# Seven half products in place of eight for the first feed-forward layers, with the weight sums on GpSimd and all low parts on VectorE

## The chip, the cores and the metric

The kernel runs on one core of a Trainium2 chip. A core has a matrix engine (TensorE, PE in the rows; its weight loads are PEld), VectorE (DVE), ScalarE (ACT), GpSimd (POOL) and a queue that issues transfers (SP). Each engine works through its own instructions in order; semaphores hold one back until another has finished. The metric is the device time of one execution in microseconds, lower is better.

## The reference

The program is a small hybrid language model in float32: one block on 512 tokens, then two blocks on 528 (16 meta tokens are put in front), width 1024. Only the feed-forwards matter here. Cut to them:

```python
def sqrelu_mlp(hn, w1, w2):            # block 1: w1 1024 x 4096
    u = hn @ w1
    u = jnp.square(jax.nn.relu(u))
    return u @ w2

def swiglu(h, w_in, w_out):            # blocks 2 and 3: w_in 1024 x 5632
    gate, up = jnp.split(h @ w_in, 2, axis=-1)
    return (jax.nn.silu(gate) * up) @ w_out

h = h + sqrelu_mlp(rmsnorm(h, norm_ff_g[l]), w_ff1[l], w_ff2[l])
h = h + swiglu(rmsnorm_2(h, norm_ffn[i]), ffn_w_in[i], ffn_w_out[i])
```

Ahead of them stand a mixer (SSD and attention), a cross attention, a gated linear attention and a sparse attention.

## The kernel before

Activations lie transposed in SBUF: partitions are channels (8 tiles of 128), the free dimension is tokens. The residual is h. TensorE multiplies in a reduced float32 format, and to keep the accuracy every operand is split into a high and a low part; a product is three passes, high x high, high weights x low activations, low weights x high activations.

Weights come in 155 units of 128 x 2048 values (1 MB), in a fixed order of layers (table LAYERS). A feed-forward unit holds two output tiles of 128 channels: 8 input tiles x 256 columns. Each unit passes three stages in two alternating buffers: SP loads w_raw (when the split of two units earlier is done), ScalarE copies w_raw to w_hi (split_hi, L363), VectorE writes w_lo = w_raw - w_hi (split_lo, L370). While TensorE computes a unit, ScalarE and VectorE split the next one. In some layers of the middle GpSimd does the subtraction instead.

TensorE's work is pe_linear (L451): per unit and output tile 8 input tiles x 3 passes, into one of two PSUM slots (lin), with 512 tokens as one matmul, with 528 as two halves of 264. The semaphore lin_done counts tiles, lin_taken the slots read.

The three feed-forwards are cut into parts: ff1a, ff2a to ff1d, ff2d (4 units each, 512 tokens), up0a, dn0a, up0b, dn0b, up0c, dn0c (8, 4, 8, 4, 6, 4 units, 528 tokens) and up1a to dn1c (the same with 512). Behind each tile of ff1 ScalarE takes the relu out of PSUM (L1691), VectorE squares it (L1708), ScalarE and VectorE split it into x_hi and x_lo (L1693, L1710). In up, a unit holds one gate tile and one up tile: VectorE scales the gate (L2036), ScalarE applies silu (L2017), VectorE multiplies by the up tile (L2040), and the result is split (L2019, L2044). The second layers add to h (L546, L549).

The norm in front of a feed-forward is applied late: the layer that ends the preceding mixer (w_xo, g_out, a_out) adds to h tile by tile, and behind each tile ScalarE writes v_hi = gain x h (L602) and the squares (L614), VectorE writes v_lo (L619), GpSimd adds up the squares (L634). TensorE sums them over partitions, ScalarE and VectorE make the reciprocal root (L684, L703) beside the first unit, and it multiplies the results.

Of the kernel before, what the change touches and what calls it, by code (L numbers as in the profile page):

```python
# [17 lines left out]
F32 = mybir.dt.float32  # L18
# [55 lines left out]

class Linear:


    def __init__(self, row, unit0, tile0):
        self.name, self.units, self.kc, self.tpu, self.n, self.token_major = row
        self.unit0, self.tile0 = unit0, tile0  # L80
        self.tiles_end = tile0 + self.units * self.tpu
        self.last = row is LAYERS[-1]

# [46 lines left out]
def build(nc, weights, x_t, mem_t, meta_t, cols, consts, w_a2b, rel_t, rel_dram, out):  # L130
# [4 lines left out]
    with ctx:  # L135
# [118 lines left out]
        after_v.close()  # L254
        sb("v_place", [P, 2, KD, T2])

# [74 lines left out]

        def for_units(eng, L, body, peel=False):
# [4 lines left out]
            if L.units % 2 == 0 and L.units // 2 - peel >= 2 and not L.last:  # L337
# [17 lines left out]
        def split_hi(act, unit, i, tiles_before):  # L355


            s = unit % 2
# [6 lines left out]
        def split_lo(dve, unit, i, does):  # L365

            s = unit % 2
# [111 lines left out]
        def act_splits(act, L, after=None):  # L479
            def unit(j, i):  # L480
                next_hi(act, L, j, i)
                if after is not None and is_first(j, i):
                    after()
            for_units(act, L, unit, after is not None)
# [31 lines left out]
        def dve_residual(dve, L, scale=None, N=None, after=None, scale2=None, after_first=None, splits_from=0):  # L516
            base = KD * residual_layers.index(L.name)

            def unit(j, i):
# [4 lines left out]
                for m in range(L.tpu):  # L524
                    slot, before, n = L.tile(j, m, i)
# [31 lines left out]
        def act_residual(act, L, N, after=None, splits_from=0):  # L557
# [3 lines left out]
            def unit(j, i):  # L561
# [4 lines left out]
                for m in range(L.tpu):  # L566
                    t, par = (2 * i + j) * L.tpu + m, (j * L.tpu + m) % 2
# [12 lines left out]
        class LaterNorm:  # L580
            def __init__(self, n, eps, first, tile, gain, hi, lo, slots=(0,), square_scale=None, tokens=(),
                         k=KD, to=None, bank=0, roots=None):
# [7 lines left out]
                self.idx, self.bank = len(later_norms), bank  # L590
                self.tiles0 = sum(N.k for N in later_norms)
# [11 lines left out]

        def act_operand(act, N, t, par):
            if N.hi is not None:
# [1071 lines left out]

        def act_relu2(act, L, after=None):
            base = hidden0[L.name]

            def unit(j, i):
                next_hi(act, L, j, i)
                if after is not None and is_first(j, i):
                    after()
                for m in range(2):
                    slot, _, n = L.tile(j, m, i)
                    t = 4 * i + 2 * j + m
                    r, sq = tmp[:, m, 0:S1], tmp[:, 2 + m, 0:S1]
                    act.wait_ge(sem("lin_done"), n + 1)

                    nc.scalar.activation(r, psum_tile(slot, S1), ACT.Relu).then_inc(sem(f"lin_taken{slot}"), 1)  # L1691
                    act.wait_ge(sem("u_made"), base + t + 1)
                    nc.scalar.activation(one(u_hi, t, 0, S1), sq, ACT.Copy).then_inc(sem("u_hi"), 1)  # L1693
            for_units(act, L, unit, after is not None)

        def dve_relu2(dve, L, after=None):
            base = hidden0[L.name]

            def unit(j, i):
                next_lo(dve, L, j, i)  # L1700
                if after is not None and is_first(j, i):
# [1114 lines left out]
```

## Time and profile before

| | |
|---|---|
| median of 3 runs | 2085.11 us (2080.94 to 2085.74) |
| profiled execution | 2085.97 us, its span 2083.9 us |
| TensorE, weight loads busy | 2007.6 us (96%), 1719.7 us (83%) |
| VectorE, ScalarE, GpSimd busy | 1055.4 (51%), 745.3 (36%), 249.3 us (12%) |
| mean granted TensorE clock | 0.978 |
| weights moved | 155 x 1 MB, 84 GB/s over the span |

The span runs from the first to the last instruction. Busy means that at least one instruction of the engine is running; matmuls overlap each other, so their rate is read from their starts. In timelines a row is start, duration, engine, line, operation, output and inputs, and in brackets the idle time before it with what ended it. A row of a stretch is its window, its length, the busy us and instructions of TensorE, of its weight loads, of VectorE, ScalarE and GpSimd, then the granted clock, the share of the transfer engines and GB/s. The granted clock is the share of TensorE's full speed that it was given.

### The profile page before, as it was taken

The numbers are of one execution on the slowest core, as the hardware profiler recorded it, in microseconds if no ns is written. First come the engines' busy times: TensorE is split into PE (matmuls) and PEld (weight loads), VectorE is DVE, ScalarE is ACT, GpSimd is POOL, SyncE is SP. The second block draws the span as 40 slices with busy tenths as digits, with TensorE's granted clock in tenths as the row PEclk, the third lists the DMA queues.
The fourth block names the chain that finished last, engine by engine and source line by source line (L and its number), as shares of the span: only waits on it lengthen the run. The fifth ranks groups of instructions, "written<-read, shape, count | busy, mean of one in ns | idle before, by whom it ended". The sixth has DMA issues, their size and how long they took to land.

```text
span 2083.9 us, 28508 instructions
## 1 busy us (share of the span) xinstructions
PE 2007.6 (96%) x11498; PEld 1719.7 (83%) x11498; DVE 1055.4 (51%) x1353; ACT 745.3 (36%) x941; POOL 249.3 (12%) x208
## 2 busy tenths in 40 slices
PE   8999989999999999999999999999997899999996
PEld 6788766788888878999999999998884588888885
DVE  6668765544444544133443434346887444434435
ACT  4449734423132443223332222224444432222222
POOL 2012230200000210013200000001254010000001
PEclk9999999999999998998999999999998899999998
DMA  4223111222222221111222222223121022222221
GB/s 174 101 81 113 62 60 61 81 101 81 101 101 81 101 82 54 68 41 41 81 82 101 82 101 81 102 81 121 61 92 32 21 101 82 100 101 82 100 101 61
DMA packets 27823, 174.67 MB, mean 84 GB/s; under 512 B 4409, under 2 KB 4537, under 8 KB 7762
## 3 DMA queue, kind: packets, MB, share of 16 engines
q1 hardware_dynamic: 25680, 167.32, 22.6%
q0 software_dynamic: 1888, 5.90, 0.9%
q8 instruction: 71, 1.16, 0.2%
q14 instruction: 22, 0.18, 0.0%
q10 hardware_dynamic: 162, 0.10, 0.0%
HBM read 171.19 MB, written 4.78 MB: 84 GB/s over the span
## 4 chain that ended last, share of the span: by engine, by line
issue 58%; PE 30%; POOL 4%; DVE 3%; ACT 3%; DMA 1%; SPq 0%; POOLq 0%; DVEq 0%; ACTq 0%
PE lin L451 18%; POOL squares L634 3%; PE aux L2278 1%; PE aux L1307 1%; DMA w_raw<-in_weights 1%; PE lin L1509 1%; PE lin L1262 1%; ACT w_hi L363 1%; PE lin L2248 1%; PE aux L2262 1%; POOL w_lo L370 1%; PE aux L1291 1%; POOL r_t L1952 1%; PE aux L2126 1%; PE aux L2274 0%
## 5 line engine op out<-in xcount | busy, mean ns | idle before, releaser
L451 PE MATMUL lin<-v_hi,w_hi 128*128 128x264 f32 (+1 forms) x1664 | 555.6, 334 | 2.6 <-DVE gq_t L1772 1.4
L451 PE MATMUL lin<-v_hi,w_lo 128*128 128x264 f32 (+1 forms) x1664 | 553.3, 333 | 0.0
L451 PE MATMUL lin<-v_lo,w_hi 128*128 128x264 f32 (+1 forms) x1664 | 552.0, 332 | 0.0
L370 DVE TENSOR_TENSOR w_lo<-w_raw,w_hi 128x2048 fp32r<-128x2048 f32 (+1 forms) x144 | 328.5, 2281 | 184.5 <-ACT w_hi L363 184.2
L451 PE MATMUL lin<-x_hi,w_hi 128*128 128x512 f32 (+1 forms) x1160 | 408.4, 352 | 13.4 <-DVE tmp L546 6.5
L451 PE MATMUL lin<-x_hi,w_lo 128*128 128x512 f32 (+1 forms) x1160 | 406.7, 351 | 0.0
L451 PE MATMUL lin<-x_lo,w_hi 128*128 128x512 f32 (+1 forms) x1160 | 406.3, 350 | 0.0
L363 ACT ACTIVATE w_hi<-w_raw 128x2048 fp32r<-128x2048 f32 (+1 forms) x155 | 293.0, 1890 | 279.8 <-PE lin L451 269.1
L451 PEld LDWEIGHTS lin<-v_hi,w_hi 128*128 128x128 f32 x1664 | 315.2, 189 | 35.8 <-issue 3.1
L451 PEld LDWEIGHTS lin<-v_lo,w_hi 128*128 128x128 f32 x1664 | 315.1, 189 | 32.0 <-issue 0.5
L451 PEld LDWEIGHTS lin<-v_hi,w_lo 128*128 128x128 f32 x1664 | 314.9, 189 | 30.7
L451 PEld LDWEIGHTS lin<-x_hi,w_hi 128*128 128x128 f32 x1160 | 219.4, 189 | 47.8 <-DVE tmp L546 7.4
L634 POOL TENSOR_TENSOR squares<-squares,tmp 128x512 f32<-128x512 f32 (+2 forms) x72 | 96.5, 1341 | 1306.9 <-ACT tmp L614 1304.3
L451 PEld LDWEIGHTS lin<-x_lo,w_hi 128*128 128x128 f32 x1160 | 219.4, 189 | 30.4 <-issue 0.2
L451 PEld LDWEIGHTS lin<-x_hi,w_lo 128*128 128x128 f32 x1160 | 219.4, 189 | 29.9
L2040 DVE TENSOR_TENSOR tmp<-tmp,lin 128x528 f32<-128x528 f32 (+1 forms) x44 | 30.6, 696 | 212.1 <-PE lin L451 212.1
L2019 ACT ACTIVATE x_hi<-tmp 128x528 f32 (+3 forms) x44 | 28.1, 640 | 218.6 <-DVE tmp L2040 218.6
L546 DVE TENSOR_TENSOR tmp<-lin,scale_d 128x512 f32<-128x512 f32 (+1 forms) x56 | 39.0, 696 | 96.1 <-PE lin L451 96.1
L370 POOL TENSOR_TENSOR w_lo<-w_raw,w_hi 128x2048 fp32r<-128x2048 f32 x11 | 51.0, 4632 | 296.5 <-ACT w_hi L363 296.5
L2017 ACT ACTIVATE tmp<-tmp 128x528 f32<-128x528 f32 (+1 forms) x44 | 28.1, 639 | 143.6 <-DVE tmp L2036 143.6
L549 DVE TENSOR_TENSOR h<-h,tmp 128x512 f32 (+3 forms) x88 | 65.1, 740 | 10.4 <-DVE tmp L546 9.0
L451 PE MATMUL lin<-w_hi,v_hi 128*128 128x256 f32 x240 | 69.6, 290 | 0.0
(391 smaller groups left out, 2408.1 us busy)
## 6 DMA issues: line engine op xcount, KB each, us to landing
w_raw<-in_weights SPq DMA_DIRECT2D x155, 1024.0 KB, 4.8
rel_by_distance<-rel_by_distance POOLq DMA_DIRECT2D x1, 2599.5 KB, 20.9
rel_bias<-rel_by_distance POOLq DMA_DIRECT2D x8, 264.0 KB, 3.0
h<-in_x_t SPq DMA_DIRECT2D x4, 512.0 KB, 8.2
out_t<-h SPq DMA_DIRECT2D x4, 512.0 KB, 2.8
o_t<-in_mem_t POOLq DMA_DIRECT2D x1, 1024.0 KB, 5.1
cst<-in_consts SPq DMA_DIRECT2D x1, 512.0 KB, 9.8
col<-in_cols ACTq DMA_DIRECT2D x1, 67.0 KB, 5.8
```

The source lines that it names most:

```text
L363: nc.scalar.activation(w_hi[:, s, 0:n], w_raw[:, s, 0:n], ACT.Copy).then_inc(sem("w_hi_ready"), 1)
L370: does.tensor_tensor(w_lo[:, s, 0:n], w_raw[:, s, 0:n], w_hi[:, s, 0:n].bitcast(F32), ALU.subtract).then_inc(sem("w_lo_ready"), 1)
L451: last = nc.tensor.matmul(o, a, b, start=(k % (L.kc // k_banks) == 0 and p == 0), stop=((k + 1) % (L.kc // k_banks) == 0 and p == 2))
L546: nc.vector.tensor_tensor(out_t, psum_tile(slot, L.n), like_psum(scale, L.n), ALU.mult)\
L549: nc.vector.tensor_tensor(ht, ht, out_t, ALU.add).then_inc(sem("h_added"), 1)
L634: nc.gpsimd.tensor_tensor(acc, acc, tmp[:, s, 0:N.n], ALU.add).then_inc(sem("square_added"), 1)
L1262: mm = nc.tensor.matmul(lin[1][64 * (hd % 2):64 * (hd % 2) + 64, 1, P * j:S1], v_tok[:, j, 64 * hd:64 * hd + 64], w_att[:, SB_AT[j]:SB_AT[ ...
L1291: mm = nc.tensor.matmul(o, memory_part(xp_, k)[:, m * P:m * P + P], wp[:, k, :], start=(k == 0 and q == 0), stop=(k == KD - 1 and q == 2))
L1307: mm = nc.tensor.matmul(o, wp[:, k, t % 4 * P:t % 4 * P + P], xp_[:, k, 0:S1], start=(k == 0 and r == 0), stop=(k == 3 and r == 2))
L2017: nc.scalar.activation(g, g, ACT.Silu).then_inc(sem("gate_silu"), 1)
L2019: nc.scalar.activation(one(u_hi, t, 0, L.n), tmp[:, 2 + j, 0:L.n], ACT.Copy)\
L2040: nc.vector.tensor_tensor(like_psum(u, L.n), like_psum(g, L.n), psum_tile(up, L.n), ALU.mult)\
```

## The change

The first layers (ff1, up0, up1: 16 + 22 + 22 units) are computed as a 2 x 2 block product with seven multiplications instead of eight. A unit's weights are four blocks of 512 columns: a11, a12, a22, a21 (input half x output tile, 4 input tiles each). The tokens are halved. From the blocks GpSimd makes four sums, in place in w_raw and in a new w_sum (single, 1536 columns): s3 = a21 - a11, a21 = a21 + a22, s2 = a21 - a11, s4 = a12 - s2. ScalarE copies high parts in four pieces (512, 1024, 512, and the 1536 of w_sum to ws_hi), VectorE subtracts all low parts in the same four pieces (ws_lo the last). The activations need sums as well: per operand tile VectorE makes second halves, and three combinations vt from tiles t and t - 4.

TensorE (pe_quads) makes seven products p1 to p7 per unit, each 4 tiles x 3 passes with half the tokens, in seven PSUM banks. VectorE puts them together: top (behind p6 and p2), mid (p5, p7), low (p4), last (p3). p1, p6, p2 of the next unit wait for top, p7, p5, p4 for low, p3 for last. The units' loops are written out.

```diff
+        def quad_sum(pool, unit, step):
+            q = quad_seq[unit]
+            a11, a12, a22, a21 = (w_block(w_raw, unit, x, x + 1) for x in range(4))
+            s3, s2, s4 = (w_sum[:, x * BLOCK_W:(x + 1) * BLOCK_W] for x in range(3))
+            if step == 0:
+                pool.wait_ge(sem(f"w_loaded{unit % 2}"), 16 * (unit // 2 + 1))
+                if q:
+                    pool.wait_ge(sem("w_lo_ready"), quad_units[q - 1] + 1)
+            else:
+                pool.wait_ge(sem("quad_sum"), 4 * q + step)
+            out_t, x, y, op = ((s3, a21, a11, ALU.subtract), (a21, a21, a22, ALU.add),
+                               (s2, a21, a11, ALU.subtract), (s4, a12, s2, ALU.subtract))[step]
+            nc.gpsimd.tensor_tensor(out_t, x, y, op).then_inc(sem("quad_sum"), 1)
...
+        def quad_lo(dve, unit, part):
...
+            elif part == 3:
+                dve.wait_ge(sem("w_hi_ready"), unit + 1)
+                nc.vector.tensor_tensor(ws_lo[:, unit % 2, :], w_sum[:, :], ws_hi[:, unit % 2, :].bitcast(F32),
+                                        ALU.subtract).then_inc(sem("w_lo_ready"), 1)
...
+            j = t - 4
+            t3, t2, t4 = (vt_raw[:, x, j, 0:hf] for x in range(3))
+            dve.wait_ge(sem("quad_gained"), 4 * N.quads0 + j + 1)
+            link(dve, nc.vector.scalar_tensor_tensor(t3, h_half(N, j, 1), N.gain(j), v_raw[:, t, hf:n],
+                                                     ALU.mult, ALU.subtract))
+            link(dve, nc.vector.scalar_tensor_tensor(t2, h_half(N, j, 0), N.gain(j), t3, ALU.mult, ALU.subtract))
+            nc.vector.tensor_tensor(t4, v_raw[:, t, 0:hf], t2, ALU.subtract).then_inc(sem("quad_raw"), 1)
...
+        QUAD_STEADY = ("p1", "p6", "p2", "p7", "p5", "p4", "p3")
+        QUAD_FIRST = ("p1", "p5", "p2", "p6", "p4", "p7", "p3")
...
+        def dve_quad_top(dve, L, t):
+            hf = L.n // 2
+            dve.wait_ge(sem("quad_done"), quad_done(L.unit0 + t, "p6", "p2"))
+            dve.wait_ge(sem("quad_s1"), quad_seq[L.unit0 + t] + 1)
+            nc.vector.tensor_tensor(tmp[:, 0:2, 0:hf], spread_row(tmp[:, 0, hf:2 * hf]), aux[:, 1:3, 0:hf],
+                                    ALU.add)\
+                .then_inc(sem("quad_top"), 1)
...
+            for t in range(L.units):
+                if t:
+                    squared(t - 1)
+                next_quad_lo(dve, L, t, (0, 1))
+                if t:
+                    low(t - 1)
+                dve_quad_top(dve, L, t)
+                next_quad_lo(dve, L, t, (2,))
+                if after is not None and t == 0:
+                    after()
+                dve_quad_mid(dve, L, t)
+                next_quad_lo(dve, L, t, (3,))
+                dve_quad_low(dve, L, t)
```

VectorE in a unit of ff1 before (tmp<-tmp is the square, x_lo the low part of the result, w_lo the split of the next unit):

```order
L370 TENSOR_TENSOR w_lo<-w_raw,w_hi 128x2048
L1708 TENSOR_TENSOR tmp<-tmp 128x512
L1710 TENSOR_TENSOR x_lo<-tmp,x_hi 128x512
L1708 TENSOR_TENSOR tmp<-tmp 128x512
L1710 TENSOR_TENSOR x_lo<-tmp,x_hi 128x512
```

And in one round after, from last to low (L1983 last, L2030 the squares, L402 to L417 the weights, L1960 top, L1968 mid, L1975 low):

```order
L1983 TENSOR_TENSOR tmp<-tmp,lin 128x256
L2030 SCALAR_TENSOR_TENSOR tmp<-tmp 128x512 x2
L402 TENSOR_TENSOR w_lo<-w_raw,w_hi 128x512
L407 TENSOR_TENSOR w_lo<-w_raw,w_hi 128x1024
L2037 TENSOR_TENSOR x_lo<-tmp,x_hi 128x512 x2
L2041 ISA
L1960 TENSOR_TENSOR tmp<-tmp,aux 128x2x256
L412 TENSOR_TENSOR w_lo<-w_raw,w_hi 128x512
L1968 TENSOR_TENSOR tmp<-tmp,lin 128x2x256
L417 TENSOR_TENSOR ws_lo<-w_sum,ws_hi 128x1536
L1975 TENSOR_TENSOR tmp<-tmp,lin 128x512
```

Five instructions have become twelve; the split, one instruction ahead of the tiles, now lies in four places between them.

VectorE in w_xo, the last layer ahead of ff1, per operand tile (one of 4 to 7) before:

```order
L530 TENSOR_TENSOR h<-h,lin 128x512
L533 ISA
L619 SCALAR_TENSOR_TENSOR v_lo<-h,col,v_hi 128x512
L530 TENSOR_TENSOR h<-h,lin 128x512
L533 ISA
```

and after, with the piece of the first quad unit's weights (L407) that stands between two tiles:

```order
L638 TENSOR_TENSOR h<-h,lin 128x512
L641 ISA
L753 SCALAR_TENSOR_TENSOR vt_raw<-h,col,v_raw 128x256
L755 SCALAR_TENSOR_TENSOR vt_raw<-h,col,vt_raw 128x256
L756 TENSOR_TENSOR vt_raw<-v_raw,vt_raw 128x256
L759 TENSOR_TENSOR v_lo<-v_raw,v_hi 128x512
L762 TENSOR_TENSOR vt_lo<-vt_raw,vt_hi 128x3x256
L407 TENSOR_TENSOR w_lo<-w_raw,w_hi 128x1024
L638 TENSOR_TENSOR h<-h,lin 128x512
```

One v_lo has become five instructions and a piece of the weights.

GpSimd stood idle through ff1 before; after, its queue has, behind the sums of squares of the norm, four additions for every unit:

```order
L797 TENSOR_TENSOR squares<-squares,tmp 128x512 x4
L372 TENSOR_TENSOR w_sum<-w_raw 128x512
L372 TENSOR_TENSOR w_raw<-w_raw 128x512
L372 TENSOR_TENSOR w_sum<-w_raw 128x512
L372 TENSOR_TENSOR w_sum<-w_raw,w_sum 128x512
L372 TENSOR_TENSOR w_sum<-w_raw 128x512
```

These four repeat up to the last unit of the part d of ff1, and likewise in up0 and up1.

## Rows read from the trace of the kernel before

**Rows 1.** The page: busy us (share of the span) and instructions of each engine.
```profile
PE 2007.6 (96%) x11498; PEld 1719.7 (83%) x11498; DVE 1055.4 (51%) x1353; ACT 745.3 (36%) x941; POOL 249.3 (12%) x208
```

**Rows 2.** Busy time by stretch: a part of ff1 and ff2, of up0.
```profile
600.00:640.00 40.00, 40.00 (x174) 32.35 (x173) 17.45 (x20) 9.44 (x7) 0.00 (x0) 1.00 0.30 105
1100.00:1150.00 50.00, 50.00 (x414) 50.00 (x413) 21.29 (x19) 13.75 (x12) 0.00 (x0) 1.00 0.24 84
```

**Rows 3.** Timeline of VectorE, splits in ff1 and an addition to h.
```profile
485.62 2.29 DVE L370 TENSOR_TENSOR w_lo<-w_raw,w_hi 128x2048 fp32r<-128x2048 f32 x1 [0.63 <-ACT w_hi L363]
...
507.91 2.29 DVE L370 TENSOR_TENSOR w_lo<-w_raw,w_hi 128x2048 fp32r<-128x2048 f32 x1 [0.86 <-ACT w_hi L363]
...
616.30 0.69 DVE L549 TENSOR_TENSOR h<-h,tmp 128x512 f32 x1 [0.17 <-DVE tmp L546]
```

**Rows 4.** Timeline of VectorE in up0, the same step five units apart.
```profile
1064.26 0.70 DVE L2040 TENSOR_TENSOR tmp<-tmp,lin 128x528 f32<-128x528 f32 x1 [5.20 <-PE lin L451]
...
1122.52 0.70 DVE L2040 TENSOR_TENSOR tmp<-tmp,lin 128x528 f32<-128x528 f32 x1 [5.13 <-PE lin L451]
```

**Rows 5.** Timeline of TensorE, matmuls of 256 columns, 35 starts apart.
```profile
829.76 0.28 PE L451 MATMUL lin<-w_hi,v_lo 128*128 128x256 f32 x1
...
833.90 0.28 PE L451 MATMUL lin<-w_hi,v_hi 128*128 128x256 f32 x1
```

**Rows 6.** Groups by line and shape: busy us, mean ns, idle before.
```profile
L1708 DVE TENSOR_TENSOR tmp<-tmp 128x512 f32<-128x512 f32 x32 | 22.1, 692 | 55.0 <-ACT tmp L1691 54.9
L370 DVE TENSOR_TENSOR w_lo<-w_raw,w_hi 128x2048 fp32r<-128x2048 f32 x138 | 317.9, 2304 | 176.9 <-ACT w_hi L363 176.7
L370 DVE TENSOR_TENSOR w_lo<-w_raw,w_hi 128x1536 fp32r<-128x1536 f32 x6 | 10.6, 1758 | 7.5 <-ACT w_hi L363 7.5
L363 ACT ACTIVATE w_hi<-w_raw 128x1536 fp32r<-128x1536 f32 x6 | 8.8, 1472 | 0.0
L602 ACT ACTIVATE v_hi<-h,col 128x512 fp32r<-128x512 f32 x24 | 17.4, 724 | 61.6 <-DVEq L533 40.3 <-DVE h L549 21.3
```

**Rows 7.** Timelines of VectorE, then GpSimd, the same microseconds.
```profile
703.73 0.75 DVE L619 SCALAR_TENSOR_TENSOR v_lo<-h,g_fin_mix,v_hi 128x512 fp32r<-128x512 f32 x1 [0.86 <-ACT v_hi L602]
704.62 0.69 DVE L546 TENSOR_TENSOR tmp<-lin,rstd 128x512 f32<-128x512 f32 x1
705.35 0.83 DVE L549 TENSOR_TENSOR h<-h,tmp 128x512 f32<-128x512 f32 x1
...
709.93 2.71 DVE L370 TENSOR_TENSOR w_lo<-w_raw,w_hi 128x2048 fp32r<-128x2048 f32 x1 [2.04 <-ACT w_hi L363]
...
704.23 1.41 POOL L634 TENSOR_TENSOR squares<-squares,tmp 128x512 f32<-128x512 f32 x1 [316.22 <-ACT tmp L614]
705.79 1.55 POOL L634 TENSOR_TENSOR squares<-squares,tmp 128x512 f32<-128x512 f32 x1 [0.16 <-POOL squares L634]
...
709.20 1.30 POOL L634 TENSOR_TENSOR squares<-squares,tmp 128x512 f32<-128x512 f32 x1 [0.16 <-POOL squares L634]
```

**Rows 8.** Timelines of VectorE, then GpSimd, in the attention.
```profile
237.47 1.48 DVE L1421 TENSOR_TENSOR stay_lo<-stay,stay_hi 128x1280 fp32r<-128x1280 f32 x1
238.87 1.78 DVE L619 SCALAR_TENSOR_TENSOR x_lo<-o_t,col,x_hi 128x512 fp32r<-128x512 f32 x1
...
237.63 2.47 POOL L2457 TENSOR_TENSOR squares<-squares,tmp 128x512 f32<-128x512 f32 x1 [6.70 <-ACT tmp L614]
```

**Rows 9.** Timeline of VectorE, end of w_xo and first unit of ff1.
```profile
376.05 0.68 DVE L530 TENSOR_TENSOR h<-h,lin 128x512 f32<-128x512 f32 x1
377.57 0.75 DVE L619 SCALAR_TENSOR_TENSOR v_lo<-h,col,v_hi 128x512 fp32r<-128x512 f32 x1 [0.85 <-ACT v_hi L602]
378.24 0.68 DVE L530 TENSOR_TENSOR h<-h,lin 128x512 f32<-128x512 f32 x1
...
387.66 3.35 DVE L703 RECIPROCAL scale_d<-scale_d 128x512 f32<-128x512 f32 x1 [1.02 <-ACT scale_d L684]
```

**Rows 10.** Busy time by stretch, columns as in rows 2, around a wait of TensorE.
```profile
284.00:288.00 4.00, 1.53 (x4) 1.25 (x5) 3.07 (x4) 0.83 (x2) 0.00 (x0) 0.81 0.65 246
```

More of the change, by code:

```diff
@@ L1713, in dve_relu2, with squared, low @@
-            for_units(dve, L, unit, after is not None)
+            def squared(t):
+                dve_quad_last(dve, L, t)
+                for m in range(2):
+                    r = tmp[:, 1 + m, 0:S1]
+                    nc.vector.scalar_tensor_tensor(tmp[:, 3 - m, 0:S1], r, 0.0, r, ALU.max, ALU.mult)\
+                        .then_inc(sem("u_made"), 1)
+            def low(t):
+                for m in range(2):
+                    k = 2 * t + m
+                    dve.wait_ge(sem("u_hi"), base + k + 1)
+                    nc.vector.tensor_tensor(one(u_lo, k, 0, S1), tmp[:, 3 - m, 0:S1], one(u_hi, k, 0, S1).bitcast(F32),
+                                            ALU.subtract).then_inc(sem("u_lo"), 1)
+                slot = L.tile(t % 2, 1, t // 2)[0]
+                dve.wait_ge(sem("u_lo"), base + 2 * t + 2)
+                nc.vector.engine_nop().then_inc(sem(f"lin_taken{slot}"), 1)
@@ L2023, in dve_swiglu @@
+            for t in range(L.units):
+                next_quad_hi(act, L, t, (0,))
+                if t:
+                    silu(t - 1)
+                act_quad_s1(act, L, t)
+                next_quad_hi(act, L, t, (1,))
+                if t:
+                    high(t - 1)
+                if after is not None and t == 0:
+                    after()
+                next_quad_hi(act, L, t, (2, 3))
+            silu(L.units - 1)
+            high(L.units - 1)
         def dve_swiglu(dve, L, after=None):
@@ new lines, in dve_swiglu @@
+            for t in range(L.units):
+                if t:
+                    gate(t - 1)
+                next_quad_lo(dve, L, t, (0,))
+                if t:
+                    made(t - 1)
+                next_quad_lo(dve, L, t, (1, 2))
+                if t:
+                    low(t - 1)
+                dve_quad_top(dve, L, t)
+                if after is not None and t == 0:
+                    after()
+                dve_quad_mid(dve, L, t)
+                next_quad_lo(dve, L, t, (3,))
+                dve_quad_low(dve, L, t)
@@ L2049, in pe_swiglu @@
+            gate(L.units - 1)
+            made(L.units - 1)
+            low(L.units - 1)
         def pe_swiglu(pe, n, N):
@@ L2602, in _ @@
             pool_attend(pool)
-            pool_squares(pool, l_ffn1, l_ffn1.idx)
+            pool_quad_squares(pool, l_ffn1, layer["up1a"].unit0, {4: (0, 1), 5: (2, 3)})
+            pool_quad_units(pool, ["up1" + part for part in "abc"], 1)
             pool_squares(pool, l_fin, l_fin.idx)
```

390 lines of the change are left out of this document (311 added, 79 removed).

## The prediction

> **What bounds the kernel now.** I read the busy line of the page first: TensorE is busy 96% of the span, VectorE 51%, ScalarE 36%, GpSimd 12% [rows 1]. Over the feed-forward stretches TensorE has no gap at all, at a granted clock of 1.00 [rows 2], so there the time is the number of matmuls times their spacing. The split of each weight unit (w_lo) repeats once per unit: two units lie between 485.62 and 507.91 us, that is 11.14 us for 48 matmuls of 512 columns, 232 ns each [rows 3]. With 528 tokens five units take 1122.52 - 1064.26 = 58.26 us, 11.65 us for 96 matmuls of 264 columns, 121.4 ns each [rows 4]. A matmul of 256 moving columns is in the trace too: 35 steps in 833.90 - 829.76 us, 118.3 ns [rows 5]. VectorE is busy 17.45 of 40 and 21.29 of 50 us there, 43%, and mostly waits for TensorE, so today its order costs nothing.
>
> **What the change takes from TensorE.** 60 units (16 of ff1, 22 of up0, 22 of up1) have 7 products x 4 tiles x 3 passes = 84 matmuls of half the tokens. At 256 columns 84 x 118.3 = 9.94 us against 11.14 (38 units), at 264 columns 84 x 121.4 = 10.19 against 11.65 (22 units). If TensorE alone decided, that were 38 x 1.20 + 22 x 1.46 = 78 us less. The question is whether the others hand over a unit every 10 us.
>
> **What it puts on VectorE, per unit of ff1.** 512 columns take 0.69 us, 2048 take 2.30, 1536 take 1.76 [rows 6], so 1.05 ns a column: 1024 take 1.23 and 256 take 0.42. Weights: 0.69 + 1.23 + 0.69 + 1.76 = 4.37 (before 2.30). Putting the products together: three of 512 and one of 256, 2.49. Two squares at the 0.75 of a scalar_tensor_tensor [rows 7], 1.50; two low parts, 1.39. Sum 9.75 us. Three of these wait for VectorE's own result, at 0.17 each (the idle time of the h addition behind tmp [rows 3]): 10.25. For the swiglu units 4.37 + 2.49 + three of 0.69 to 0.71 = 9.0, and four such waits: 9.6. By itself that is about TensorE's new 9.9 to 10.2.
>
> **What GpSimd adds to it: the term that decides.** GpSimd makes four additions of 512 columns per unit, 1.30 us each where nothing holds them up, 0.16 apart [rows 7]. The trace shows that an addition there and a VectorE instruction with both inputs in SBUF never run together. [Rows 7]: VectorE's v_lo ends at 704.48; GpSimd's addition, started at 704.23, ends at 705.64, 1.16 behind it. VectorE's h addition, started at 705.35, ends at 706.18, 0.54 (512 columns) behind 705.64. GpSimd's next ends at 707.34, again 1.16 behind 706.18. The w_lo that starts at 709.93 takes 2.71 instead of 2.29, since GpSimd's ends at 710.50. VectorE's L546 at 704.62 has one input in PSUM and takes its 0.69 beside a running addition. So every instruction on SBUF alone excludes GpSimd: weights, squares, gate, low parts; the four that read PSUM don't. The two take turns: at 237.63 the addition waits for one VectorE instruction and runs before the next, which takes 1.78 instead of 0.75 [rows 8]. A turn costs VectorE 1.16 less the 0.16 in which its instruction starts anyway, 1.0 us. The Trainium skill's page "SBUF — State Buffer" (section "SBUF: two separate sides") has the rule: the pair of ports that VectorE and GpSimd share is an exclusive lock for the whole instruction. The trace agrees to 0.01 us. The same page of the Trainium skill says that the order of issue decides who blocks; that VectorE always comes first is part of rival 3.
>
> Now the round of one unit, in the new order (the second piece of order in the section on the change). GpSimd may start the sums of the next unit only when ws_lo has been written. Behind ws_lo VectorE puts two products together (0.69 and 0.42, PSUM) while the first addition runs: no cost. Then squares, w_lo and w_lo meet additions 2, 3 and 4, at 1.0 each: 10.25 + 3.0 = 13.2 us per ff1 unit; in swiglu w_lo, made and w_lo: 9.6 + 3.0 = 12.6. The other side of the same ring, in which nothing may start before the former: four additions with two delays 6.6 to 7, ScalarE's 1536 columns 1.47 [rows 6], ws_lo 1.76, and before it the low parts, top, w_lo and mid at 3.3: about 13 too. Both give more than TensorE's 9.9 and also than the 11.14 and 11.65 of before. Bounds: with no turn paid the unit takes 10.2, with four paid 14.2; I take three, as the order shows only the first beside PSUM work.
>
> **Layers.** A layer's first unit has its weights ready from the layer before and VectorE's first round lacks squares and low parts, so two units run at TensorE's pace. The last round splits an ordinary unit (2.30 for 4.37, no sums): 11.4 to 11.7, ff1 leaving 0.2 behind, swiglu 1.4 to 2.1 until the last low part reaches the down projection. ff1b, c, d: 2 x 9.94 + 13.2 + 11.65 + 0.2 = 44.9 each against 44.6: +1 together. up0b: 2 x 10.19 + 5 x 12.6 + 11.4 + 1.4 = 96.2 against 93.2; up0c: 20.4 + 3 x 12.6 + 11.4 + 1.9 = 71.5 against 69.9. up1b: 19.9 + 5 x 12.5 + 11.1 + 1.6 = 95.1 against 89.1; up1c: 19.9 + 37.5 + 11.1 + 2.1 = 70.6 against 66.8. Sum of these seven: +15.
>
> **The three first layers.** Today an operand tile costs VectorE 0.69 + 0.75 and passes every 2.19 us (376.05 to 378.24) [rows 9], under the 2.78 of TensorE per tile of w_xo. New, each of tiles 4 to 7 has h 0.69, ScalarE's gained copy 0.73 [rows 6] with 0.1 of hand-over, 0.46 + 0.46 + 0.42 with 0.16 behind each, 0.69 with most of a GpSimd turn (the squares sum, 0.8) and 768 columns 0.96: about 6 us, in order, and the parts of the weights (4.37) stand between them. In w_xo that is 28 us for four tiles against TensorE's 11: TensorE waits some 7 us inside w_xo (its PSUM slots aren't emptied) and in the first ff1 unit until tile 7 is split, about 15 us after its start; five products, the sum of squares and ScalarE's root follow: 23 us against 11.6. In g_out and a_out the tiles are 5.8 and 5.6 us apart, but the weights make VectorE late too: 22 against 12.5. The second unit then has the reciprocal, 3.35 [rows 9], in front of its ws_lo: 16 us each. ff1a: 7 + 23.3 + 16.3 + 13.2 + 11.7 + 0.2 against 45.0: +26.7. up0a: 22 + 15.8 + 5 x 12.6 + 11.4 + 1.4 = 113.6 against 94.2: +19.4. up1a: 22.4 + 15.7 + 62.5 + 11.1 + 1.6 = 113.3 against 90.2: +23. Sum +69. Bounds: -3 if all of it were hidden as now (half of each layer's gain), +95 if each turn in it were lost whole.
>
> **Clock.** After waits of this length it drops: 1.53 us of work in 284 to 288, with 0.81 granted over these 4 us [rows 10], so the clock stood at its lower level, 1.2 of 2.4 GHz, for some 1.5 us of them. Behind the waits of 4 to 7 us in three first units I add 5 us in all (0 to 15); inside an ordinary unit the waits are 1.2 to 1.7 us and VectorE, not TensorE, is behind.
>
> **Sum.** 2085.97 (profiled execution; the median is 2085.11, 0.9 lower, which I leave aside) + 15 + 69 + 5 = 2175 us.
>
> **Rivals.**
> 1. Faster: the two engines don't exclude each other here (the new additions read other tensors, and VectorE's waits may fall where GpSimd works). Then a unit takes 9.94 to 10.46, the seven later layers gain 48, the first layers lose about 20: 2057. Turning point: under one paid turn per unit. Against it are the four exact ends of [rows 7]. 9%.
> 2. The ordinary units as forecast, but the operand tiles hidden far better (ScalarE ahead, tiles spread): +30 to +45 in all, 2122. The 2.19 us ring of today, of which 0.85 is waiting, speaks for some slack. 15%.
> 3. GpSimd loses more turns: a fourth paid one in the 30 units that VectorE bounds, and in the first layers, +38: 2213. Were VectorE always first, three additions would stand bare at 1.46 instead of a turn of 1.0, with the 1.47 of the copy behind them: 2.8 more in 30 units, +84: 2259. [Rows 8] show it getting the turn between two VectorE instructions. 14%.
> 4. The savings and the losses cancel, within 0.3% (6 us, what a measurement of this kernel can tell from nothing): 2%.
>
> The forecast has 60%. Its own range is 2145 to 2205; the range over the cases, leaving out rival 1 and the starved end, is 2100 to 2228. Faster 0.09, same 0.02, slower 0.89.
>
> **What would show it.** In the profile after: ordinary ff1 units at 13 us, swiglu units at 12.5; VectorE busy near 95% there, with w_lo of 512 columns at about 1.7 and of 1024 at 2.2; GpSimd's additions at 1.3 to 1.8; TensorE stopping twice per unit, before the first product (for the top addition) and before the second (for ws_lo), 1.2 to 1.7 us each; the ff2 and down units unchanged. The first ff1 unit 20 us or more. I am wrong if w_lo keeps 0.69 and 1.23, if TensorE runs gapless at 10 us, or if the first layers lose under 10 us each.

## The result and the profile after

The changed kernel takes 2145.84 us (median of 4 runs, 2144.06 to 2148.80) against 2084.74 of the kernel before in the same comparison: a ratio of 1.030, 95% interval 1.028 to 1.032. It is slower by 61 us; the forecast was 89. The profiled execution's span is 2146.9 us (before 2083.9).

The busy line of the page after, to be read against [rows 1]:

```profile
PE 1971.0 (92%) x12602; PEld 1745.4 (81%) x12602; DVE 1539.5 (72%) x1845; ACT 863.8 (40%) x1185; POOL 625.8 (29%) x448
```

TensorE has only 37 us less to do (in narrow pieces, and part of them at a lower clock), while VectorE has 484 us more and GpSimd 377. Busy time by stretch of the kernel after, columns as in [rows 2] (us; busy time and instructions of PE, PEld, DVE, ACT, POOL; PEclk, DMA share, GB/s): one round of ff1, two rounds of up0, and the first unit of up0:

```profile
512.00:524.50 12.50, 11.79 (x99) 11.58 (x99) 12.25 (x13) 5.13 (x7) 6.16 (x4) 1.00 0.23 85
1112.50:1137.00 24.50, 21.65 (x170) 20.67 (x168) 23.92 (x23) 10.37 (x15) 12.37 (x8) 1.00 0.24 86
1070.00:1090.00 20.00, 14.76 (x88) 14.07 (x88) 18.99 (x16) 11.21 (x14) 8.73 (x5) 0.83 0.15 53
```

In the stretches of [rows 2] TensorE had no gap and VectorE was busy 43%. Now VectorE is busy 98% and it is TensorE that has gaps: the bound has moved. What one round consists of, the timeline of VectorE in the kernel after (start, duration, engine, line), from one first sum of products (L1960) to the next:

```profile
512.41 0.69 DVE L1960 TENSOR_TENSOR tmp<-tmp,aux 128x512 f32<-128x512 f32 x1
513.01 0.68 DVE L412 TENSOR_TENSOR w_lo<-w_raw,w_hi 128x512 fp32r<-128x512 f32 x1
513.62 0.68 DVE L1968 TENSOR_TENSOR tmp<-tmp,lin 128x512 f32<-128x512 f32 x1
514.21 1.75 DVE L417 TENSOR_TENSOR ws_lo<-w_sum,ws_hi 128x1536 fp32r<-128x1536 f32 x1
515.88 0.68 DVE L1975 TENSOR_TENSOR tmp<-tmp,lin 128x512 f32<-128x512 f32 x1
516.66 0.42 DVE L1983 TENSOR_TENSOR tmp<-tmp,lin 128x256 f32<-128x256 f32 x1
517.12 2.54 DVE L2030 SCALAR_TENSOR_TENSOR tmp<-tmp 128x512 f32<-128x512 f32 x2
519.58 1.78 DVE L402 TENSOR_TENSOR w_lo<-w_raw,w_hi 128x512 fp32r<-128x512 f32 x1
521.28 2.31 DVE L407 TENSOR_TENSOR w_lo<-w_raw,w_hi 128x1024 fp32r<-128x1024 f32 x1
523.51 1.28 DVE L2037 TENSOR_TENSOR x_lo<-tmp,x_hi 128x512 fp32r<-128x512 f32 x2
524.91 0.69 DVE L1960 TENSOR_TENSOR tmp<-tmp,aux 128x512 f32<-128x512 f32 x1
```

And GpSimd's four additions in the same round:

```profile
516.11 1.30 POOL L372 TENSOR_TENSOR w_sum<-w_raw 128x512 f32<-128x512 f32 x1 [6.10 <-DVE ws_lo L417]
517.48 1.63 POOL L372 TENSOR_TENSOR w_raw<-w_raw 128x512 f32<-128x512 f32 x1
519.19 1.62 POOL L372 TENSOR_TENSOR w_sum<-w_raw 128x512 f32<-128x512 f32 x1
520.89 1.62 POOL L372 TENSOR_TENSOR w_sum<-w_raw,w_sum 128x512 f32<-128x512 f32 x1
```

Read the two together. The first addition runs beside L1975 and L1983, which read PSUM, and takes its bare 1.30. The second ends at 519.11, inside the pair of squares (L2030); the third at 520.81, and the w_lo of 512 columns that started at 519.58 ends at 521.36, 0.55 later; the fourth at 522.51, and the w_lo of 1024 columns ends at 523.59, 1.08 later. Both end their own bare length (0.68 and 1.22), less 0.13, after the addition. That is the picture of [rows 7], three times per unit. Over the whole kernel, groups by line (busy us, mean ns, idle before):

```profile
L407 DVE TENSOR_TENSOR w_lo<-w_raw,w_hi 128x1024 fp32r<-128x1024 f32 x60 | 127.6, 2127 | 0.0
...
L402 DVE TENSOR_TENSOR w_lo<-w_raw,w_hi 128x512 fp32r<-128x512 f32 x60 | 98.2, 1637 | 0.5
L412 DVE TENSOR_TENSOR w_lo<-w_raw,w_hi 128x512 fp32r<-128x512 f32 x60 | 43.4, 724 | 0.3
```

L402 and L412 are the same operation on the same shape; the one that meets an addition takes 1637 ns, the one that doesn't 724. Beside the turns, the chain through GpSimd and ScalarE doesn't hold VectorE up. ScalarE's copy of the sums starts right behind the fourth addition:

```profile
522.54 1.49 ACT L395 ACTIVATE ws_hi<-w_sum 128x1536 fp32r<-128x1536 f32 x1 [1.69 <-POOL w_sum L372]
```

It ends at 524.03, and VectorE comes to the next ws_lo (L417) at 526.71, 2.7 us later, without an idle gap. What TensorE waits for in the half products (L1921), the largest entries of its waits (total us, times, longest):

```profile
PE aux L1921 <- DVE ws_lo L417: 37.0, 39, 4.2
PE aux L1921 <- DVE tmp L1960: 23.6, 30, 1.0
...
PE lin L1921 <- DVE w_lo L412: 9.0, 2, 4.8
```

All three are VectorE. In the layers in front of the feed-forwards it waits for VectorE too, since the operand tiles are made there. Timeline of TensorE in w_xo (the idle time before is in brackets), and at the start of ff1a:

```profile
376.49 0.51 PE L556 MATMUL lin<-x_hi,w_hi 128*128 128x512 f32 x1 [2.07 <-DVE h L638]
383.11 0.80 PE L556 MATMUL lin<-x_hi,w_hi 128*128 128x512 f32 x1 [3.54 <-DVE h L638]
...
396.35 0.55 PE L1921 MATMUL lin<-v_hi,w_hi 128*128 128x256 f32 x1 [6.23 <-issue]
```

For the last row the profile names no releaser. In the kernel this product waits until the last PSUM slot of w_xo has been read. VectorE's last addition to h (L638), which reads it, starts at 395.58 and takes 0.67, so it ends 0.10 us before the product starts.

Where the time went, by TensorE's first matmul of each layer in the two traces: w_xo +7.7, ff1a +15.3, up0a +14.9 and the layers ahead of it +2.0, up1a +18.8 and the layers ahead of it +2.4; ff1b, c and d 0.0 each, up0b -0.1, up0c -2.1, up1b +2.9, up1c +0.3. So 61 us lie in and before the three first layers and 1 us in the seven later ones, where the shorter products and the longer rounds cancel. The 2.0 and 2.4 us ahead of up0a and up1a are weak evidence: in the traces of the variants below these two stretches differ from before by -0.6 to +6.6 and by -9.6 to +0.4 us.

### The profile page after: what moved, and what is told of

The parts are those of the page before. It is cut to its first block, busy times and chain, and to the rows that moved or that the text cites. A ratio compares the mean times of both kernels' runs of the same rounds, so it can differ in the third digit from the quotient of the medians.

```text
span 2146.9 us, 31250 instructions
## 1 busy us (share of the span) xinstructions
PE 1971.0 (92%) x12602; PEld 1745.4 (81%) x12602; DVE 1539.5 (72%) x1845; ACT 863.8 (40%) x1185; POOL 625.8 (29%) x448
## 4 chain that ended last, share of the span: by engine, by line
PE 43%; DVE 29%; issue 18%; POOL 5%; ACT 3%; DMA 1%; DVEq 0%; POOLq 0%; SPq 0%; ACTq 0%
PE lin L556 27%; DVE w_lo L402 3%; PE lin L1921 3%; DVE w_lo L407 3%; PE aux L1921 3%; POOL squares L818 3%; DVE tmp L2385 2%; DVE tmp L1968 1%; DVE scores L2538 1%; DVE tmp L1960 1%; DVE best L2533 1%; DVE tmp L1975 1%; PE aux L2640 1%; DVE tmp L2381 1%; DVE ws_lo L417 1%
## 5 line engine op out<-in xcount | busy, mean ns | idle before, releaser
L372 POOL TENSOR_TENSOR w_sum<-w_raw 128x512 f32<-128x512 f32 x120 | 176.7, 1473 | 603.6 <-DVE ws_lo L417 340.4
L475 DVE TENSOR_TENSOR w_lo<-w_raw,w_hi 128x2048 fp32r<-128x2048 f32 (+1 forms) x84 | 195.2, 2324 | 125.1 <-ACT w_hi L466 124.7
L466 ACT ACTIVATE w_hi<-w_raw 128x2048 fp32r<-128x2048 f32 (+1 forms) x95 | 177.8, 1871 | 145.0 <-PE lin L556 135.2
L1921 PE MATMUL aux<-v_hi,w_hi 128*128 128x256 f32 (+1 forms) x480 | 140.1, 292 | 27.6 <-DVE tmp L1960 23.6
L1921 PE MATMUL aux<-v_lo,w_hi 128*128 128x256 f32 (+1 forms) x480 | 137.4, 286 | 0.0
L1921 PE MATMUL aux<-v_hi,w_lo 128*128 128x256 f32 (+1 forms) x480 | 137.0, 285 | 0.0
L407 DVE TENSOR_TENSOR w_lo<-w_raw,w_hi 128x1024 fp32r<-128x1024 f32 x60 | 127.6, 2127 | 0.0
L1921 PEld LDWEIGHTS aux<-v_hi,w_hi 128*128 128x128 f32 x480 | 92.8, 193 | 33.7 <-issue 28.9
L556 PE MATMUL lin<-v_hi,w_hi 128*128 128x264 f32 (+1 forms) x352 | 116.1, 330 | 2.6 <-DVE gq_t L2116 1.4
L556 PE MATMUL lin<-v_hi,w_lo 128*128 128x264 f32 (+1 forms) x352 | 113.5, 323 | 0.0
L556 PE MATMUL lin<-v_lo,w_hi 128*128 128x264 f32 (+1 forms) x352 | 113.3, 322 | 0.0
L1921 PE MATMUL aux<-vt_hi,ws_hi 128*128 128x256 f32 (+1 forms) x240 | 74.7, 311 | 37.1 <-DVE ws_lo L417 37.0
## 6 DMA issues: line engine op xcount, KB each, us to landing
rel_by_distance<-rel_by_distance POOLq DMA_DIRECT2D x1, 2599.5 KB, 20.9
```

Source lines behind the costliest of these rows:

```text
L372: nc.gpsimd.tensor_tensor(out_t, x, y, op).then_inc(sem("quad_sum"), 1)
L407: nc.vector.tensor_tensor(w_block(w_lo, unit, 1, 3), w_block(w_raw, unit, 1, 3), w_block(w_hi, unit, 1, 3).bitcast(F32), ALU.subtract)\
L466: nc.scalar.activation(w_hi[:, s, 0:n], w_raw[:, s, 0:n], ACT.Copy).then_inc(sem("w_hi_ready"), 1)
L475: does.tensor_tensor(w_lo[:, s, 0:n], w_raw[:, s, 0:n], w_hi[:, s, 0:n].bitcast(F32), ALU.subtract).then_inc(sem("w_lo_ready"), 1)
L556: last = nc.tensor.matmul(o, a, b, start=(k % (L.kc // k_banks) == 0 and p == 0), stop=((k + 1) % (L.kc // k_banks) == 0 and p == 2))
L1921: mm = nc.tensor.matmul(bank[:, b, 0:hf], wp[:, k * P:(k + 1) * P], xp_, start=(k == 0 and p == 0), stop=(k == 3 and p == 2))
```

## The experiments

The kernel before, measured beside them on the same chip, had a median of 2080.6 to 2084 us. Ratios are to it. Differences between kernels of different comparisons are taken from the ratios, at 2082 us for 1.

**1. What do the additions cost through what they read?** GpSimd's four additions became four writes of zeros over 1536 columns: about as long, the same waits and order, but they read nothing (the sums of the weights are left out).

```
-            nc.gpsimd.tensor_tensor(out_t, x, y, op).then_inc(sem("quad_sum"), 1)
+            nc.gpsimd.memset(w_sum[:, :], 0.0).then_inc(sem("quad_sum"), 1)
```

> GpSimd's four additions per unit become four memsets of w_sum (1536 columns each, about as long as an addition, but reading nothing from SBUF); the weight sums are left out. Chain, order and waits are the same. Theory A (each addition excludes VectorE's instructions on SBUF, three turns of about 1 us per unit on a full VectorE): w_lo of 512 and 1024 columns fall from 1.64 and 2.13 us to 0.69 and 1.23, ordinary units from 12.5 and 12.1 to 10 us (TensorE's pace), the whole to 2040 to 2060 us, below the kernel before. Theory B (the single w_sum makes a ring of additions, copy and ws_lo that is too long, whoever reads): the ring is as long as now, units stay at 12 to 12.5 us, 2140 us or more.

Measured: 2056.3 us, ratio 0.988 (0.986 to 0.991), by the ratios 86 us under the changed kernel. Two groups of VectorE and the timeline of GpSimd in this run:

```profile
L407 DVE TENSOR_TENSOR w_lo<-w_raw,w_hi 128x1024 fp32r<-128x1024 f32 x60 | 73.4, 1223 | 22.7 <-ACT w_hi L387 22.7
...
L402 DVE TENSOR_TENSOR w_lo<-w_raw,w_hi 128x512 fp32r<-128x512 f32 x60 | 41.1, 685 | 0.5
```

```profile
1075.76 5.71 POOL L372 MEMSET w_sum<- 128x1536 f32 x4 [3.79 <-DVE ws_lo L417]
```

GpSimd is busy for 5.71 us behind ws_lo, nearly as long as the 6.4 from 516.11 to 522.51 above, and yet the w_lo parts are back at 685 and 1223 ns, the bare times. The length of GpSimd's chain isn't what costs; what an addition has and a write of zeros lacks, its reads of SBUF beside VectorE's, is. The rounds fell to TensorE's own pace, 9.95 us in ff1 and 10.2 in up0. The rival that the chain of GpSimd, ScalarE and ws_lo sets the round falls, as the 2.7 us of slack in the changed kernel also say.

**2 and 3. The additions on VectorE: all four, or all but the first.** If turns are the cost, an addition on VectorE (0.69) is cheaper than one on GpSimd that takes a turn.

```
-            for step in range(4):
+            for step in ():            # all on VectorE;   (0,): the first on GpSimd
                 quad_sum(pool, unit, step)
...
             if part == 0:
+                for step in (0, 1, 2, 3):                # and (1, 2, 3)
+                    quad_sum(dve, unit, step, nc.vector)
                 dve.wait_ge(sem("quad_w_hi"), 3 * q + 1)
```

> All four sums of a unit on VectorE ahead of its first weight part, none on GpSimd. Theory A: a unit of VectorE loses three turns of 0.94 us and gains four instructions of 0.61: 12.5 becomes 12.1 in ff1 and 12.05 becomes 11.7 in up; with 30 such units and the three first layers 2125 to 2143 us. Theory B: the ring loses GpSimd's 6.2 us and becomes 3.7 shorter, VectorE has no turns to pay, units near 11 us or below, under 2110.

> The first sum of a unit stays on GpSimd, the other three go to VectorE. Theory A says the first addition costs nothing, as it runs beside the two instructions on PSUM behind ws_lo, and each of the others costs 0.94 there against 0.61 on VectorE: 12.5 becomes 11.5, 12.05 becomes 11.1, the whole about 2110 us (2100 to 2120). If the turn were an average slowing by a busy GpSimd and not a lock, the gain would be spread evenly: a quarter less loss per addition and 0.61 more work per sum, 12.3 and 11.9, 2135 us or more.

Measured: 2123.48 us, ratio 1.021 (1.018 to 1.025), and 2099.16 us, ratio 1.009 (1.006 to 1.012). Both lie under the range expected (2125 to 2143 and 2100 to 2120), by 1.5 and 0.8 us. A turn had been priced at 0.94 and costs 1.15 on average (3.44 for three, below), so taking turns away gave more. Rounds: 11.84 us in ff1 with all on VectorE, 11.26 with the first on GpSimd, 12.5 in the changed kernel. VectorE with all four, the squares, the first and the last addition, and the first w_lo of a round:

```profile
504.50 1.29 DVE L2033 SCALAR_TENSOR_TENSOR tmp<-tmp 128x512 f32<-128x512 f32 x2
505.71 0.68 DVE L372 TENSOR_TENSOR w_sum<-w_raw 128x512 f32<-128x512 f32 x1
...
507.88 0.69 DVE L372 TENSOR_TENSOR w_sum<-w_raw,w_sum 128x512 f32<-128x512 f32 x1
508.49 0.68 DVE L404 TENSOR_TENSOR w_lo<-w_raw,w_hi 128x512 fp32r<-128x512 f32 x1
```

The four take 508.49 - 505.71 = 2.78 us of the 11.84, so VectorE's round without them is 9.06. The squares cost 1.29 here and 2.54 in the changed kernel, the w_lo 0.68 against 1.78. VectorE does the four additions faster than it can let GpSimd do three of them.

**4. What do the new operand tiles cost?** The sums of the activations aren't made; the products read the plain operand, and VectorE makes one low part per tile as in the kernel before.

```
-                         x = [v[:, ("p7", "p6", "p4").index(name), k, 0:hf] for v in (vt_hi, vt_lo)]
+                         x = [v[:, k, 0:hf] for v in (v_hi, v_lo)]
...
```

> The activations' sums and their splits are left out: each operand tile is prepared as in the kernel before (one v_hi, one v_lo), the products read v in place of vt. Weight sums and products stay. Measures the operand part of the three first layers: w_xo back to 2.8 us per tile (7 to 8 us less), first units 22 and 21 to 15 and 11.5, in all 30 us less, 2115 us (2105 to 2125). If the first layers' loss were that of the weights alone, under 8 us less.

Measured: 2117.93 us, ratio 1.018 (1.016 to 1.021), 24 us under the changed kernel by the ratios. The rounds of the ordinary units stayed at 12.5 and 12.1, so the 24 us are those of the layers in front of the feed-forwards and the first layers. The pace of 2.8 us per tile in w_xo, part of the expectation, did not come back: the additions to h are 3.9 and 5.1 us apart (378.02, 381.94, 387.02), with a part of the weights between them each time.

**5. Do the two add up?** Edits 1 and 4 together (the sums of weights and of activations are both left out).

> Both cuts together: GpSimd only writes zeros in place of the four additions, and the sums of the activations aren't made (products read the plain operand). If the two costs add up, the turns (-88 us in the run that only wrote) and the operand tiles (-28 us in the run with plain operands) give 2118 - 89 = 2029 us, 2015 to 2040, 2.5% under before: what seven half products can give TensorE, less the second unit of each first layer, which keeps the reciprocal of 3.35 us. If the operand tiles cost only through turns with GpSimd's sums, little is left to gain: 2045 to 2056.

Measured: 2032.79 us, ratio 0.976 (0.974 to 0.979); 2029 was expected. The turns and the operand tiles are two costs beside each other: by the ratios 86 and 24 us alone, 112 together. What is left, some 50 us under before, is what TensorE's narrower products bring in the seven later layers, 48 us by the traces. The three first layers and what lies ahead of them lose 61 us in the changed kernel, 17 without the additions' reads, 34 with plain operands and nothing with both edits (2 us gained).

**6. Four additions in the kernel before.** GpSimd makes four additions of 512 columns per unit of the feed-forwards, on data that nothing reads.

```
+                    pool.wait_ge(sem("w_lo_ready"), unit)
...
+                    for out_t, x, y in ((s3, s2, s4), (s2, s3, s4), (s4, s3, s2), (s3, s2, s4)):
+                        link(pool, nc.gpsimd.tensor_tensor(out_t, x, y, ALU.add))
```

> The kernel before, with the four additions of 512 columns per feed-forward unit added on GpSimd, on data that nobody reads (the result is unchanged). If the exclusion between GpSimd and VectorE costs only where VectorE is what the unit waits for: the splits (w_lo, 2048 columns) grow from 2.30 us by about one turn, to some 3.2, but VectorE was busy 43% of a unit, so the time stays within 0.3% of before. If four more GpSimd instructions per unit cost something by themselves (traffic that slows TensorE's operands, semaphores, the clock): over 0.5% slower, and the 11.14 us per unit grow.

Measured: 2080.12 us, ratio 0.9997 (0.998 to 1.001). One part of the expectation was wrong: the splits kept 2.29 us, because the additions start behind a split and end before the next. They met the addition to h instead, or a square (1.50 at 655.07). Timelines of VectorE and of GpSimd in this run:

```profile
633.00 1.27 DVE L552 TENSOR_TENSOR h<-h,tmp 128x512 f32 x1 [0.16 <-DVE tmp L549]
...
639.75 2.29 DVE L373 TENSOR_TENSOR w_lo<-w_raw,w_hi 128x2048 fp32r<-128x2048 f32 x1 [0.48 <-ACT w_hi L366]
```

```profile
631.04 5.75 POOL L636 TENSOR_TENSOR w_sum<-w_sum 128x512 f32<-128x512 f32 x4 [47.72 <-DVE w_lo L373]
```

A turn is paid (1.27 in place of 0.69) and costs nothing, for VectorE was busy 11.46 of 23 us there (628 to 651) and TensorE all 23. The additions have no price of their own above the interval's 0.2%; they have one where VectorE is the bound.

**7 and 8. Place the additions.** If a turn is paid only against instructions with both inputs in SBUF, a second addition is free wherever VectorE reads PSUM for a microsecond. The order of the sums was turned so that one of them (a21 + a22, in place) needs only the loaded block; GpSimd makes it when VectorE starts on L1960's sum, the next (a21 - a11) behind ws_lo, and VectorE the two that follow from it. In ff1 the last w_lo was put ahead of that sum, so that the two PSUM instructions stand together. All sums are made, the third as s2 - a22.

```
+                if unit in quad_opened:
+                    pool.wait_ge(sem("quad_opened"), quad_opened[unit])
...
+            out_t, x, y, op = ((a21, a21, a22, ALU.add), (s2, a21, a11, ALU.subtract),
+                               (s3, s2, a22, ALU.subtract), (s4, a12, s2, ALU.subtract))[step]
...
+            if L.unit0 + t + 2 in quad_opened:
+                nc.vector.engine_nop().then_inc(sem("quad_opened"), 1)
```

> A full kernel: two of the four additions on GpSimd, each placed where VectorE reads PSUM (one behind ws_lo as in the run with one on GpSimd, the other, which only needs the loaded block, when VectorE starts to put the first products together), two on VectorE. By the exclusion, whose turn is paid only against instructions with both inputs in SBUF, the second addition is free as well: a unit loses another 0.65 us against the run with one on GpSimd (11.26 to 10.6 in ff1, 11.03 to 10.4 in up), in some 40 units: about 2072 us, 2062 to 2082, level with before or 0.8% under it. If the windows don't hold (the addition starts late and meets ws_lo or w_lo), it pays a turn of 0.94 instead of the 0.69 saved: 2100 to 2110.

The control has two on GpSimd and two on VectorE as well, without the placing and in the changed kernel's order of sums (experiment 3 with steps 0 and 1 on GpSimd):

> As the kernel with two additions in windows, two on GpSimd and two on VectorE, but without the placing: both additions start one behind the other after ws_lo, in the changed kernel's order. If the place of an addition sets its price, the second one meets the squares or the swiglu gate (both inputs in SBUF) and pays one turn of 0.94 us where the run with one on GpSimd paid 0.69 on VectorE: a unit is 0.2 to 0.3 us longer than there (11.5 in ff1, 11.25 in up), 2099 + 44 x 0.25 = 2110 us, 2103 to 2116, ratio 1.010 to 1.017. If only the number of additions on GpSimd counts and the placing is worth nothing: as the run in windows, 2066 to 2076 us, ratio under 1.

Measured: placed 2070.86 us, ratio 0.994 (0.991 to 0.996); unplaced 2119.61 us, ratio 1.016 (1.014 to 1.019). A round is 10.53 and 10.27 us placed, 11.6 and 11.6 unplaced. Timeline of the placed one in up0, VectorE and then GpSimd:

```profile
1100.45 0.70 DVE L1974 TENSOR_TENSOR tmp<-tmp,aux 128x528 f32<-128x528 f32 x1
1101.26 0.70 DVE L1982 TENSOR_TENSOR tmp<-tmp,lin 128x528 f32<-128x528 f32 x1
1101.88 1.75 DVE L428 TENSOR_TENSOR ws_lo<-w_sum,ws_hi 128x1536 fp32r<-128x1536 f32 x1
1103.55 0.70 DVE L1989 TENSOR_TENSOR tmp<-tmp,lin 128x528 f32<-128x528 f32 x1
...
1104.82 0.82 DVE L2395 TENSOR_TENSOR tmp<-tmp,scale_d 128x528 f32<-128x528 f32 x1
```

```profile
1100.54 1.29 POOL L381 TENSOR_TENSOR w_raw<-w_raw 128x512 f32<-128x512 f32 x1 [5.74 <-DVEq L1971]
1103.78 1.30 POOL L381 TENSOR_TENSOR w_sum<-w_raw 128x512 f32<-128x512 f32 x1 [1.95 <-DVE ws_lo L428]
```

Both take the bare 1.29 and 1.30, and the VectorE instructions that read PSUM beside them their bare time. The second one ends at 1105.08, inside the scaling of the gate (both inputs in SBUF), which takes 0.82 in place of 0.71. So the place is nearly free, at 0.1 us; in ff1 the pair of squares takes 1.43 there in place of 1.29. The unplaced one cost more than expected (2119.61 against at most 2116). Its VectorE and GpSimd in up0:

```profile
1108.71 0.82 DVE L2384 TENSOR_TENSOR tmp<-tmp,scale_d 128x528 f32<-128x528 f32 x1
1110.72 0.69 DVE L372 TENSOR_TENSOR w_sum<-w_raw 128x512 f32<-128x512 f32 x1 [1.19 <-POOL w_raw L372]
```

```profile
1109.05 1.64 POOL L372 TENSOR_TENSOR w_raw<-w_raw 128x512 f32<-128x512 f32 x1
```

Here VectorE's next instruction needs GpSimd's result: it waits 1.19 us, where a paid turn was priced at 0.94. In ff1 the price is a turn, the pair of squares at 2.54 again (503.33). The direction was right and the ratio is in the range given, the time above it. The expectation had priced the turn too low and had left out the wait for data. The placed kernel differs from this one in several things at once (the order of sums, the signal, the w_lo put ahead), so the 47 us between them are the worth of the placing as a whole.

**9. The reciprocal.** In the placed kernel, the reciprocal of ff1a (3.35 us) and rstd (0.69) moved from the second weight unit to behind the last.

```
-                dve_relu2(dve, layer["ff1" + part], ff_root if part == "a" else None)
+                dve_relu2(dve, layer["ff1" + part])
+                if part == "a":
+                    ff_root()
```

> The run before this one in the list, with the reciprocal (3.35 us) and the square of it (0.69) of the first layer ff1a moved from the second weight unit to behind the last one, where VectorE has slack. If VectorE's order is the path there, the second unit gets 3 to 4 us shorter and the whole 3 to 4 us: about 2068 us. If TensorE's start of the second unit was bound by the operands in any case, nothing: same as the run before it.

Measured: 2067.96 us, ratio 0.992 (0.990 to 0.995). In its trace the second unit fell from 14.43 to 10.55 us, as expected. In the total the 2.9 us of difference lie within both intervals, and the stretch between ff1d and up0a was 2.7 us longer in the profiled execution: shown in its place, not shown in the sum. It is the best of the kernels with all the computation: 0.8% under before and 78 us under the changed kernel.

A second w_sum, by which GpSimd could start without waiting for ws_lo, wasn't tried, so it stays open whether more than two additions could be placed.

## Why the prediction was right

The forecast was slower, 2175 us; 2145.84 lies 0.8 us inside its own range of 2145 to 2205. The four runs differ by more than that, so that it lies inside at all is luck. The mechanism, turns of the two engines on a full VectorE, is what the runs show. The size was too large by 28 of 89 us.

- **The exclusion decides.** Right, and now shown by taking the reads away: 86 of the changed kernel's microseconds are turns. Rival 1 (2057 us if nothing is excluded) is what experiment 1 measured, 2056.3, and in its trace the parts are there too: the seven later layers gain 47 us (48 in the working) and the first layers lose 17 (20).
- **Three turns per unit, the first addition free.** Right. No ordinary round pays a fourth one, so rival 3 falls. The turns were dearer than the 1.0 predicted: squares 2.54 - 1.29 = 1.25, w_lo 1.78 - 0.68 = 1.10, w_lo 2.31 - 1.22 = 1.09, together 3.44 us.
- **VectorE's own 10.25 us per unit.** This is the step that was mis-sized most: it measured 9.06. The durations sum to 9.38 and not 9.75 (the pair of squares 1.29, not 1.50; 0.68, not 0.69 to 0.71), and instead of 0.51 us of waiting for its own results the instructions overlap by 0.32 net: in the round above L417 starts at 514.21 with 1.75, and L1975 at 515.88. So 9.06 + 3.44 = 12.5 against 13.2; the swiglu rounds measured 12.1 and 12.0 against 12.6 and 12.5.
- **The other side of the same ring, about 13 too.** Wrong: it is near 10. The working put the low parts, top, w_lo and mid (3.3) between ScalarE's copy and ws_lo, but none of them waits for that copy. From one ws_lo to the next stand 6.4 us of additions, 1.49 of the copy and 1.75 of ws_lo itself, with 0.15 us and less between them, and 2.7 us of slack. It changes nothing in the sum, as VectorE's side was the longer one.
- **The later layers, +15.** It was +1. The rounds that VectorE bounds, one in each ff1 layer and 16 in the swiglu layers by the working, were 0.5 to 0.7 us shorter each: about 10 of the 14 us. Nearly all of the other 4 lie in the first of these rounds in each layer. Counted from TensorE's first product of one unit to that of the next it lasts 12.02 us in ff1b, 11.33 in up0b and 11.45 in up1b, less than the round of 12.5, 12.1 and 12.0. The last units with what follows them cancel: longer in ff1 (12.66 against 11.85), shorter in up0c and up1c (11.99 and 11.80 against 13.3 and 13.2). TensorE's two stops in an ordinary unit were 0.7 to 1.1 us each instead of 1.2 to 1.7.
- **The first layers +69 and the clock +5.** They came to 61 with the clock in it, so they were not hidden as rival 2 has it. An operand tile took 5.5 us instead of 6: the additions to h of four tiles start at 375.77, 382.38, 388.45 and 395.58, and the parts of the weights between them take 3.4 of these 19.8 us. TensorE waited 5.6 us in w_xo against 7. Experiment 4 prices the new tiles at 24 us. From first product to first product, the first units took 20.1, 20.9 and 21.2 us against 23.3, 22 and 22.4. ff1a measured 60.7 against 64.7, up0a 109.1 and up1a 108.8 against 113.6 and 113.3; the shorter rounds explain 2.5 us of each swiglu layer. The clock fell as said. The granted clock was 0.84 over 372 to 449 us, 0.93 over 1040 to 1110 and 0.91 over 1730 to 1790, and 1.00 before in the same layers. An estimate from these shares, 77 x 0.16 + 70 x 0.07 + 60 x 0.09, is 23 us of TensorE's full pace. That is only an upper bound for the cost, since in much of that time TensorE waits for VectorE in any case; how much of the 61 us the clock is stays open. The wait of the second unit is shown in the changed kernel by its first sums of products, the timeline of VectorE in ff1a and up0a:

```profile
406.06 0.67 DVE L1960 TENSOR_TENSOR tmp<-tmp,aux 128x512 f32<-128x512 f32 x1
423.13 0.69 DVE L1960 TENSOR_TENSOR tmp<-tmp,aux 128x512 f32<-128x512 f32 x1
...
1085.09 0.69 DVE L1960 TENSOR_TENSOR tmp<-tmp,aux 128x528 f32<-128x528 f32 x1
1100.45 0.70 DVE L1960 TENSOR_TENSOR tmp<-tmp,aux 128x528 f32<-128x528 f32 x1
```

17.07 and 15.36 us where 16 each was predicted. Of the first, 3.9 are the reciprocal and its square, by what the placed kernel gained in experiment 9.

## What to carry to other kernels

Half products save TensorE's time only if the engine that prepares them has room: cost its round with the instructions' own starts, since back to back they overlap. In these runs an addition of 512 columns on GpSimd cost VectorE at most 0.15 us where it began beside work that reads PSUM, 1.1 to 1.25 us beside work with both inputs in SBUF, and 1.2 us of waiting where VectorE needed its result at once. Three turns (3.44 us) cost more than doing all four additions on VectorE (2.78). So place such additions, or keep them on VectorE.

## What the runs showed that was not expected

Writes alone aren't excluded. Experiment 1 took this for granted and no row of before shows it: GpSimd's memsets of 1536 columns left VectorE's w_lo at its bare 685 ns. The Trainium skill's page "SBUF — State Buffer" (section "SBUF: two separate sides") says so too: a VectorE instruction with two SBUF inputs takes the shared pair only against a GpSimd instruction that reads SBUF. The traces agree on both sides of it: the additions lengthened w_lo to 1637 ns on average, and VectorE's instructions with one input in PSUM ran beside an addition at their bare 0.68 to 0.70 us.

Executions of one kernel come in lengths some 8 to 10 us apart. With two additions unplaced the runs gave 2109.0 and 2111.6, and four times 2119.6 to 2120.1. In the traces such a difference lies in the attention, whose code is the same in all kernels. The stretch between the feed-forwards, with the columns as above, of the run with one addition on GpSimd:

```profile
1407.00:1724.00 317.00, 283.64 (x1454) 226.81 (x1453) 247.04 (x494) 145.48 (x255) 94.90 (x68) 0.94 0.19 67
```

and of the run with two unplaced, profiled in one of its short executions:

```profile
1421.00:1728.00 307.00, 277.74 (x1452) 223.53 (x1451) 238.57 (x492) 145.35 (x255) 98.13 (x70) 0.96 0.20 69
```

The same work but for two matmuls, 10 us apart, TensorE's granted clock 0.94 and 0.96 on average. What sets the one or the other stays open; differences under 10 us need several runs of each kernel.
